# Pre norm of the second block: a thin time-step strip of two matmuls a k-tile, three strips side by side, and three weight refills subtracted by VectorE

## The reference, cut to what matters

```
x = first_block(...)                    # ends with rmsnorm(h, final_norm_g)
h = rms_norm(x, mix_pre_g)
proj = h @ w_in                         # u_glu: 2048 columns, dt_raw: 32 columns, ...
val, gt = split(u_glu + glu_b);  v = val * sigmoid(gt);  v = causal_depthwise_conv(v, 31 taps)
dt = softplus(dt_raw + dt_bias);  a_dt = dt * -exp(a_log);  a_cs = cumsum(a_dt) per chunk
```

## Time and profile before

| | |
|---|---|
| median of 3 runs | 1923.01 us (1921.47 to 1925.6) |
| profiled execution, its time | 1923.79 us |
| profiled execution, span | 1922.0 us |
| PE busy | 1886.4 us, 98% |
| DVE busy | 1014.7 us, 53% |
| ACT busy | 1085.4 us, 56% |
| PE clock granted, mean | 0.995 of full |

### The profile page before, as it was taken

How to read it: one execution, slowest core, us unless ns; L and a number is a source line. 1 busy time by engine, 2 the same in 40 slices (tenths; PEclk the granted TensorE clock), 3 DMA queues, 4 the chain that set the end, 5 groups by cost and what they waited for, 6 DMA issues and landing times.

```text
span 1922.0 us, 26122 instructions
## 1 busy us (share of the span) xinstructions
PE 1886.4 (98%) x9270; PEld 1549.3 (81%) x9270; DVE 1014.7 (53%) x1677; ACT 1085.4 (56%) x1512; POOL 255.8 (13%) x299
## 2 busy tenths in 40 slices
PE   7999999999999999999999999999999999999999
PEld 6877788877888888878888888888888878888886
DVE  5566663435513233358888888788633273133134
ACT  7655666534433333454589997798574544344343
POOL 0110001100111111111111111111111101111110
PEclk9999999999999999999999999999999989999999
DMA  7854468853888889859887678867888839889884
GB/s 225 197 133 109 121 171 202 182 114 103 195 194 192 192 194 196 190 135 214 178 187 190 171 170 213 205 169 174 219 186 201 184 94 210 192 194 193 194 178 113
DMA packets 94345, 339.98 MB, mean 177 GB/s; under 512 B 10488, under 2 KB 10488, under 8 KB 93984
## 3 DMA queue, kind: packets, MB, share of 16 engines
q0 software_dynamic: 42480, 153.64, 44.0%
q1 hardware_dynamic: 47232, 169.14, 30.2%
q10 hardware_dynamic: 4528, 15.81, 2.2%
HBM read 334.27 MB, written 4.28 MB: 176 GB/s over the span
## 4 chain that ended last, share of the span: by engine, by line
PE 82%; DVE 9%; ACT 3%; DMA 3%; issue 2%; ACTq 1%; DVEq 1%; SPq 0%
PE bank L386 21%; PE bank L387 21%; PE bank L388 21%; DVE ssum L2094 4%; PE bank L511 2%; PE bank L513 2%; PE bank L512 2%; PE work L466 1%; DMA wl<-in_weights 1%; PE bank L401 1%; PE bank L403 1%; PE bank L402 1%; PE work L681 1%; PE work L691 1%; PE work L531 1%
## 5 line engine op out<-in xcount | busy, mean ns | idle before, releaser
L984 ACT ACTIVATE wh<-raw 128x1024 fp32r<-128x1024 f32 x295 | 312.2, 1058 | 589.9 <-PE bank L388 500.6
L386 PE MATMUL bank<-XAh,wh 128*128 128x512 f32 x1384 | 546.1, 395 | 11.0 <-DVE XAl L1597 9.7
L388 PE MATMUL bank<-XAh,wl 128*128 128x512 f32 x1384 | 539.9, 390 | 0.0
L387 PE MATMUL bank<-XAl,wh 128*128 128x512 f32 x1384 | 539.7, 390 | 0.0
L964 POOL DMA_DIRECT2D wl<-in_weights x295 | 255.6, 867 | 1636.6 <-ACT wl L985 1600.3
L386 PEld LDWEIGHTS bank<-XAh,wh 128*128 128x128 f32 x1384 | 260.5, 188 | 68.5 <-issue 13.7
L985 ACT ACTIVATE wl<-raw 128x1024 fp32r<-128x1024 f32 x295 | 307.7, 1043 | 0.0
L388 PEld LDWEIGHTS bank<-XAh,wl 128*128 128x128 f32 x1384 | 260.3, 188 | 55.3
L387 PEld LDWEIGHTS bank<-XAl,wh 128*128 128x128 f32 x1384 | 260.6, 188 | 53.2 <-issue 0.7
L386 PE MATMUL bank<-XBh,wh 128*128 128x512 f32 x720 | 281.2, 391 | 0.4 <-DVE wl L1544 0.4
L388 PE MATMUL bank<-XBh,wl 128*128 128x512 f32 x720 | 280.2, 389 | 0.0
(11 more groups left out here) (364 smaller groups left out, 2107.4 us busy)
## 6 DMA issues: line engine op xcount, KB each, us to landing
raw<-in_weights SPq DMA_DIRECT2D x294, 512.0 KB, 6.5
wl<-in_weights POOLq DMA_DIRECT2D x287, 512.0 KB, 8.0
arena<-scratch ACTq DMA_DIRECT2D x20, 512.0 KB, 5.6
wraw<-in_weights SPq DMA_DIRECT2D x12, 512.0 KB, 7.3
raw<-in_weights SPq DMA_DIRECT2D x8, 384.0 KB, 4.4
wl<-in_weights POOLq DMA_DIRECT2D x8, 384.0 KB, 6.3
h<-in_xT SPq DMA_DIRECT2D x4, 512.0 KB, 8.0
spill<-cst ACTq DMA_DIRECT2D x8, 256.0 KB, 6.1
```

The source lines that it names most:

```text
L386: mm(bank[s][:, 0:w], hi, tile(X[0], k, w), start=(n == 0), stop=False)
L387: mm(bank[s][:, 0:w], hi, tile(X[1], k, w), start=False, stop=False)
L388: last = mm(bank[s][:, 0:w], lo, tile(X[0], k, w), start=False, stop=(n == len(kts) - 1))
L984: act_(wh[j % 4][:, :], raw[a % 2][:, :], ACT.Copy)
```

## The change

- `LOCAL` takes in strips 137, 138 and 139 (`glu` + 3 to + 5): ACT makes one pass over each instead of two, DVE subtracts, POOL issues no DMA.
- `low_beside(AT["dt"], 32)` on DVE, between the last `final_sum` and the first `cols_recip`: it copies the 32 low columns of each of the eight k-tiles of strip 133 beside the high ones, at columns 32 to 63. The same helper now serves the strip `ff`.
- `strips_abreast` runs three strips (133, 134, 135) for each k-tile, with two matmuls for the thin one (133) and three for the others.
- DVE's bias step of `dt` becomes three: copy partitions 32 to 63 of the bank, add partitions 0 to 31, add the bias.
- DVE subtracts 137 and 138 right behind `s_abs`, and 139 right behind `s_acs`.

```
-LOCAL = [AT["xo"] + n for n in range(4, 8)] + [AT["gu0"] + n for n in range(4, 7)]
+LOCAL = [AT["xo"] + n for n in range(4, 8)] + [AT["glu"] + n for n in range(3, 6)] + [AT["gu0"] + n for n in range(4, 7)]
...
-            def strips_abreast(j, count, X, xn):
+            def strips_abreast(j, count, X, xn, thin=None):
                 for n in range(j, j + count):
-                    low_ready(n)
+                    if n == thin:
+                        pe.wait_ge(sem("thin"), 2)
+                    else:
+                        low_ready(n)
                     pe.wait_ge(bank_free[n % 4], n // 4)
                 for k in range(KT):
                     pe.wait_ge(x_ready, xn[k] + 1)
-                    for s in [n % 4 for n in range(j, j + count)]:
+                    for n in range(j, j + count):
+                        s = n % 4
                         hi, lo = wh[s][:, k * P:(k + 1) * P], wl[s][:, k * P:(k + 1) * P]
                         mm(bank[s][:, :], hi, tile(X[0], k), start=(k == 0), stop=False)
-                        mm(bank[s][:, :], hi, tile(X[1], k), start=False, stop=False)
-                        last = mm(bank[s][:, :], lo, tile(X[0], k), start=False, stop=(k == KT - 1))
+                        last = mm(bank[s][:, :], hi, tile(X[1], k), start=False, stop=(n == thin and k == KT - 1))
+                        if n != thin:
+                            last = mm(bank[s][:, :], lo, tile(X[0], k), start=False, stop=(k == KT - 1))
...
-            strips_abreast(AT["dt"], 2, XA, tiles_from("pre"))
-            for n in range(1, 2 * KT):
+            strips_abreast(AT["dt"], 3, XA, tiles_from("pre"), thin=AT["dt"])
+            for n in range(2, 2 * KT):
                 strip(AT["glu"] + n, XA)
...
+            def low_beside(j, n):
+                dve.wait_ge(w_lo[j % 4], 16 * lows(j))
+                hi, lo = [a[j % 4].rearrange("p (k n) -> p k n", k=KT) for a in (wh, wl)]
+                copy(hi[:, :, 32:32 + n], lo[:, :, 0:n].bitcast(F32))
+                dve.drain().then_inc(sem("thin"), 1)
...
             final_sum(KT - 1)
             dve.drain().then_inc(ssum_rdy, 1)
+            low_beside(AT["dt"], NSH)
             cols_recip(NORM["final"])
...
             ps = taken(AT["dt"])
-            leave(TS(acs[0:NSH, :], ps[0:NSH, :], V("dt_b")[0:NSH, :], None, ALU.add), AT["dt"])
+            copy(acs[0:NSH, :], ps[32:32 + NSH, :])
+            dve.drain()
+            leave(TTop(acs[0:NSH, :], acs[0:NSH, :], ps[0:NSH, :], ALU.add), AT["dt"])
+            dve.drain()
+            TS(acs[0:NSH, :], acs[0:NSH, :], V("dt_b")[0:NSH, :], None, ALU.add)
             dve.drain()
             STT(xt[0:NSH, 0, :], acs[0:NSH, :], -1.0, acs[0:NSH, :], ALU.mult, ALU.max)
             dve.drain().then_inc(sem("s_abs"), 1)
+            for n in (3, 4):
+                sub_local(AT["glu"] + n)
             one_plus(NSH, xt[:, 0, :], xt[:, 1, :], sem("s_exp"), sem("s_one"))
...
             dve.drain().then_inc(sem("s_acs"), 1)
+            sub_local(AT["glu"] + 5)
```

More of the change, by code:

```diff
@@ L1833, in _ @@
                 elif n == 6:
[L1834 to L1838, removed]
+                    low_beside(AT["hgrn"] + n + 2, FH)
                 elif n == 9:
```

## The result

The changed kernel takes 1925.86 us (median of 20 runs, 1924.19 to 1930.06), the kernel before 1923.37 in 20 runs. The ratio is 1.0016, with a 95% interval of 1.0010 to 1.0022. By the ratio it is 3.1 us slower (1.9 to 4.2), the medians lie 2.5 us apart. That is under the 0.2% that one would call a change, and yet clear of no change.

A forecast was written before the change was run, and what follows sets the result against it. PE, busy for 98% of the span, was taken to bound the kernel. Ahead of and behind strip 138, +1.75 us of later start and +1.6 of low clock made +3.35: 1926.4 us (+0.17%), range 1922.3 to 1929.3.

The forecast's parts named there:

- The wait at bank 2: Ahead of strip 138: PE stands 3.6 us until DVE's multiply L2111 frees the bank; strip 138 starts 1.75 us later.
- dt later because two strips run beside it: At the seam's abreast part: dt's last matmul ends at 849.41 instead of 846.21, 3.2 us later.
- The chain: Softplus chain from dt's last matmul to DVE's multiply that frees bank 2: 15.55 us, 1.45 shorter than before.
- The copy beside: `low_beside` on DVE ahead of the reciprocal: a copy of 0.30 us, delaying everything behind by 0.25 us (0.15 to 0.4).
- The low clock: Behind PE's 3.6 us wait ahead of strip 138: slow matmuls cost 1.6 us, priced by 8 matmuls in 3.4 us.
- The seam in all: Sum at strip 138: 1.75 us later start plus 1.6 us of low clock, +3.35 us.
- the low clock at the start: At the seam's opening: it holds for a time, not for a count of matmuls, and costs the same as before.
- 848.5 below: Time when PE is at the last k-tile, long after DVE delivers the last two tiles by 844.60.
- Three DMAs of POOL less ... give nothing: Behind strip 138: three fewer POOL DMAs ease the queue, but PE waits for nothing there, so no gain.
- no other wait: Behind the seam: no other wait in which the 3.35 us could be won back, since DVE and ACT move with PE.
- Rival C: Start of strip 138: softplus chain stays under PE's work, 1.86 us faster, 1921.2 us; chance 0.10.
- Rival D: Strip 141's refill also late, its `raw` freed later: 0.7 to 3.2 us more, up to +6.5, 1929.6 us; chance 0.13.

The follow-up runs named there:

- the first experiment: The changed kernel with ACT's first sigmoid ahead of its wait for the scan and DVE's subtraction of 139 behind its first multiply: 1925.12 us, ratio 1.0012.
- the subtractions alone: The kernel before with only DVE's three subtractions of strips 137 to 139, dt and 134 abreast in full: 1922.85 us, ratio 0.9999.
- three full strips abreast: The kernel before with the three subtractions and three full strips abreast, dt with three matmuls a k-tile: 1925.9 us, ratio 1.0013.
- both waits mended: The changed kernel with three spare POOL DMAs, first sigmoid ahead of the scan wait, 139 rounded before it and subtracted behind the first multiply: 1922.95 us, ratio 0.9998.
- before with the sigmoid first: The kernel before with only ACT's first sigmoid moved ahead of its wait for the scan: 1924.47 us, ratio 1.0001.

## Why the prediction was right

- *The wait at bank 2.* Forecast: 3.6 us ahead of strip 138, released by L2111. Measured: 3.59 us, by the same instruction (L2127 now). That this bank is the cause is shown by the first experiment, in which the wait is 0.19 us.
- *dt later because two strips run beside it.* Shown by the pair of the subtractions alone and three full strips abreast: the same work in another order brings the wait (none, then 2.35 us) behind a chain of the same 14.5 us. Neither the thin form nor the longer bias does. In the changed kernel dt ends 3.17 us later behind strip 132 (3.2 forecast).
- *The chain.* Forecast 15.55 us, measured 15.7; the first softplus step 5.5 us behind dt, measured 5.65. The copy beside took 0.29 us (0.30).
- *The low clock.* Forecast 1.6 us from the earlier trace rows, measured 1.58 by filling the wait. The Trainium skill, page "TensorE: Matmul & The Clock Gate", section "HAM oscillation — how this bites in real kernels", tells of a kernel in which the array waits for data so long that the next k-tile starts at the low clock, each time. The traces here agree for the waits of 1.84 to 5.02 us ahead of a strip, each with slow matmuls behind it. Behind the waits of 1.0 to 1.3 us between strips (at 871.3, 917.9 and at the second norm) none of the next 30 matmuls was slow.
- *The seam in all.* Forecast +3.35, measured +3.48: 0.12 up to the first k-tile, 1.75 from there to strip 138, 1.61 behind it. The forecast held that the low clock at the start costs the same as before; it covered 9 matmuls rather than 8, 0.2 us of the 1.75, and this count is scatter. (Its "848.5 below" for PE at the last k-tile should be 848.8 by its own sum; nothing rests on it.)
- *"Three DMAs of POOL less ... give nothing", "no other wait".* This step failed. The row that it leaned on, 860 to 880 us in the earlier trace rows, says nothing of the second norm. PE had a new wait of 1.17 us at 1584.9, and 1.1 to 1.3 us there in the four experiments that dropped the three DMAs with nothing in their place; the four kernels that kept all of POOL's refills had 0.4 us or less. From the second norm to the last matmul those five took 384.0 to 385.3 us and those four 383.3 to 384.3. It is no clean rule: the kernel with one DMA less waited 1.8 us there, behind a landing of 9.4 us. With spare DMAs in the place of the three, POOL issues in time, and the wait was 1.06 us in one kernel and 0.39 in the other. So the 0.7 us of POOL's own late issue are argued from the rows and not shown, and the landings of this refill, 7.8 to 9.4 us in the profiles where PE waited for it, differ by more than that. That the whole came out right in spite of this is in part luck: the seam and the stretch behind the second norm make +4.2 us, the upper end of what the ratio allows, and the stretch between them took 1.16 us less in this execution. 0.7 us of that is less in small waits, and all of it is within the 2.3 us by which this stretch scatters over the profiles.
- *Rival C* (the chain stays hidden, 1.86 us gained) is not what happened. With both waits mended it was not seen either, though the interval of that run just reaches it: its profile has new waits for DVE and for a refill in this stage.
- *Rival D*, late refills: not in the changed kernel, but it decides two of the experiments, at strip 137 instead of 141.

## What to carry to other kernels

Running more strips side by side makes each of them finish later: if one of them heads a long chain of small steps on other engines, measure from its last matmul to the end of the step that frees the buffer which the chain holds, and compare with the work that PE has meanwhile. Then price the wait twice, once for its length and once for the low clock behind it, where rows of the kernel show one behind waits of that length. Matmuls that are saved are worth little where the other engines are nearly as full as PE: mending the waits gave the loss back, and the 1.8 us of saved matmuls could not be seen.

## What was not expected of the hardware

POOL issued the DMAs with the numbers 60, 113, 117, 174, 223, 231 and 288 of its list (counted from 0) late, 1.0 us behind ACT's pass rather than 0.3 (numbers 113 and 223: 1.6 us), though nothing that they waited for was late. It was the same numbers in ten kernels, at times that differ by up to 56 us. In the two with spare DMAs 184, 237 and 241 stood in the place of the last four. Why is open. With three DMAs fewer ahead of it number 231 fell from a place with slack, at 1525.3 us, to the first refill behind the second norm, at 1576.9. An edit can move such a hiccup to a sensitive place 700 us away.

The low clock at the start of the seam lasted for 6 to 13 matmuls, 0.2 us each, from one execution to the next of nearly the same program: a scatter of over 1 us. It does not come of the edits: the kernel before had 8, and two experiments that leave this part as it was, the subtractions alone and before with the sigmoid first, had 13 and 12.
